# Moving the statistics tile ahead of the activations in SBUF, in a two-block transformer kernel on one core

## What is computed

```python
# first block, once
h = rmsnorm(x, norm_mix_g); u = h @ w_in                 # 1024 x 5376
o_a = rwkv7_time_mix(u[:, :1792], ...)                    # 256 x 512
o_b = diff_attention(u[:, 1792:3328], ...)                # 256 x 512
g_a, g_b = split(sigmoid(u[:, 3328:]))
x = x + (g_a * (o_a @ w_proj_a) + g_b * (o_b @ w_proj_b)) @ w_out
x = x + square(relu(rmsnorm(x) @ w_ff1)) @ w_ff2          # 1024 x 4096 x 1024
x = x + (p @ w_ple) * sigmoid(rmsnorm(x) @ w_ple_gate)
x = rmsnorm(x, final_norm_g)
# second block, two layers
x = x + 0.5 * swiglu(rms_norm(x), gate, up, down)         # 1024 x 2816, twice, x 1024
x = x + mix(rms_norm(x) @ w_in_ab or w_in_cd) @ w_out_2   # attention, 16 heads of 64
x = x + 0.5 * swiglu(rms_norm(x), gate, up, down)
```

## The kernel before

| tile | from byte | modulo 256 |
|---|---|---|
| raw, hi, lo (nine of 8192 bytes) | 0 | 0 |
| X | 73728 | 0 |
| h | 81920 | 0 |
| cols, const | 98304, 98816 | 0, 0 |
| small | 110144 | 64 |
| st (1408 bytes) | 118144 | 128 |
| RB, nt, arena | 119552, 120576, 124672 | 0 |

## Time and profile before

### The profile page before, as it was taken

How to read it: one execution, slowest core, us unless ns; L and a number is a source line. 1 busy time by engine, 2 the same in 40 slices (tenths; PEclk the granted TensorE clock), 3 DMA queues, 4 the chain that set the end, 5 groups by cost and what they waited for, 6 DMA issues and landing times.

```text
span 1466.1 us, 22896 instructions
## 1 busy us (share of the span) xinstructions
PE 1439.1 (98%) x9382; PEld 1233.7 (84%) x9382; DVE 1012.8 (69%) x1339; ACT 767.8 (52%) x1044; POOL 29.6 (2%) x96
## 2 busy tenths in 40 slices
PE   7999999999999999999999999999999999999999
PEld 6999988888887788888878888888888887788887
DVE  5785667787446787647776877468774688687753
ACT  5844365554335565435675555355553456565542
POOL 0000000000001200000000000000000000000000
PEclk9999999999999999999999999999999999999999
DMA  8441124555553465554424555545555454255552
GB/s 312 160 173 60 60 88 169 202 205 196 198 200 145 145 229 175 198 197 156 165 87 145 202 199 176 197 163 211 176 198 195 147 179 146 82 203 199 178 196 86
DMA packets 35815, 249.11 MB, mean 170 GB/s; under 512 B 4096, under 2 KB 4224, under 8 KB 6144
## 3 DMA queue, kind: packets, MB, share of 16 engines
q1 hardware_dynamic: 35712, 247.65, 47.6%
HBM read 246.59 MB, written 1.05 MB: 169 GB/s over the span
## 4 chain that ended last, share of the span: by engine, by line
PE 65%; DVE 1%; ACT 1%; issue 0%; POOL 0%; DVEq 0%; ACTq 0%; POOLq 0%
PE ps L1842 19%; PE ps L1801 10%; PE ps L1841 9%; PE ps L1803 9%; PE ps L1802 9%; PE ps L1838 3%; PE ps L1839 1%; PE ps L2145 1%; PE ps L2125 1%; PE ps L1871 1%; PE ps L2134 0%; PE ps L2074 0%; DVE lo L2494 0%; PE ps L2107 0%; DVE X L2543 0%
## 5 line engine op out<-in xcount | busy, mean ns | idle before, releaser
L2494 DVE TENSOR_TENSOR lo<-raw,hi 128x2048 fp32r<-128x2048 f32 x230 | 526.3, 2290 | 237.0 <-ACT hi L2173 236.7
L2173 ACT CAST hi<-raw 128x2048 fp32r<-128x2048 f32 x230 | 439.1, 1910 | 241.2 <-PE ps L1803 238.1
L1842 PE MATMUL ps<-h,hi 128*128 128x512 f32 x1456 | 519.5, 396 | 0.0
L1841 PE MATMUL ps<-h,lo 128*128 128x256 f32 x1456 | 406.7, 279 | 0.8 <-DVE h L2518 0.8
L1842 PEld LDWEIGHTS ps<-h,hi 128*128 128x128 f32 x1456 | 273.3, 188 | 56.2
L1841 PEld LDWEIGHTS ps<-h,lo 128*128 128x128 f32 x1456 | 274.6, 189 | 10.6 <-DVE h L2518 1.1
L1801 PE MATMUL ps<-hi,a 128*128 128x512 f32 x584 | 230.3, 394 | 0.0
L1803 PE MATMUL ps<-hi,a 128*128 128x512 f32 x584 | 227.6, 390 | 0.0
L1802 PE MATMUL ps<-lo,a 128*128 128x512 f32 x584 | 227.4, 389 | 0.0
L2358 ACT COPY a<-ps 128x256 f32<-128x256 f32 x208 | 76.4, 373 | 204.3 <-PE ps L1842 198.9
L1801 PEld LDWEIGHTS ps<-hi,a 128*128 128x128 f32 x584 | 109.7, 188 | 23.7 <-issue 2.2
(11 more groups left out here) (328 smaller groups left out, 1590.2 us busy)
## 6 DMA issues: line engine op xcount, KB each, us to landing
raw<-ws SPq DMA_DIRECT2D x230, 1024.0 KB, 4.8
X<-xin SPq DMA_DIRECT2D x8, 256.0 KB, 6.3
const<-const SPq DMA_DIRECT2D x1, 1352.0 KB, 11.3
out<-X SPq DMA_DIRECT2D x4, 256.0 KB, 2.1
small<-small SPq DMA_DIRECT2D x1, 992.5 KB, 13.1
a<-row SPq DMA_DIRECT2D x1, 512.0 KB, 5.9
a<-pin SPq DMA_DIRECT2D x1, 256.0 KB, 5.1
const<-const SPq DMA_DIRECT2D x1, 64.0 KB, 2.3
```

What stands on the lines that cost most here:

```text
L1841: e.matmul(b2(sl)[:, 0, :], wl[:, k, a:a + 128], HH[:, k, :], start=False, stop=False)
L1842: t = e.matmul(b2(sl), wh[:, k, a:a + 128], h2[:, k, :, :], start=False, stop=k == 7)
L2173: e.copy(hi[j % NSPL][:, :], raw[j % NRAW][:, :]).then_inc(hi_ready, 1)
L2494: e.tensor_tensor(lo[j % NSPL][:, :], raw[j % NRAW][:, :], hi[j % NSPL][:, :].bitcast(F), ALU.subtract).then_inc(lo_ready, 1)
```

## The change

The line that allocates `st`, the small tile of row statistics and scalars, moves up by five tiles, from behind `small` to ahead of `h`. `h`, `cols`, `const` and `small` each move up by its 1408 bytes, which is 128 modulo 256. `h` begins at 83328 (128 modulo 256), `cols` and `const` too are at 128, `small` at 192, `st` at 0. `raw`, `hi`, `lo`, `X`, `RB`, `nt` and the whole arena stay where they were. No instruction is added, removed or reordered.

```diff
         X = fixed("X", [128, 2, D])
+        st = fixed("st", [128, 352])
         h2 = fixed("h", [128, 8, 2, S], R)
         HH, HL = h2[:, :, 0, :], h2[:, :, 1, :]
         cols = fixed("cols", [128, NCOL])
         const = fixed("const", [128, NK])
         small = fixed("small", [128, NS_])
-        st = fixed("st", [128, 352])
         RB = fixed("RB", [128, S])
```

## The result

Median 1470.61 us (1469.27 to 1471.65, 18 runs) against 1468.13 us before (1466.70 to 1469.25, 18 runs): a ratio of 1.002, 95% interval 1.0014 to 1.0027. The kernel became slower by about 2.5 us. The forecast was 16 us faster.

A forecast was written before the change was run, and what follows sets the result against it. The prediction took TensorE's matmuls to bound the kernel. 16.7 us saved on matmuls reading `h` and weights, less 0.7 us for waits, gave 16.0 us: from 1467.86 to 1451.9 us, by the median 1452 us, range 1429 to 1473 us.

The forecast's parts named there:

- What bounds the kernel: Whole kernel: TensorE, busy 1439.1 of 1466.1 us at full clock, sets the time through the cost of 9382 matmuls.
- The relative address matters, and only to matmuls that read both: `wide`, `cols` and `rows` on `h`: 5056 matmuls reading `h` and weights change pace; products from other tiles keep theirs.
- The rival that nothing would happen: Rival for the whole kernel: the moved address changes no pace, time stays at 1468 us; chance 0.17.
- period 128: Within the no-change rival: addresses may count modulo 128, so the new place of `h` equals the old; 1468 us.
- The price: Matmuls reading `h` and weights: each saves 3.3 ns, `rows` included, 5056 x 3.3 = 16.7 us; chance for 2.2 to 4.4: 0.50.
- The row of `ob`: `cols` on `ob`, 64 bytes off, took 117.8 ns against 120.0 on `oa`: 64 bytes worth 2.2 ns a matmul.
- The streams part wholly: Rival for matmuls on `h`: 6.7 ns saved each, as with 8-column loads, and even passes; 37.5 us, 1430.5 us; chance 0.18.
- Growth with distance: Matmuls on `h`: if savings grow with distance, 128 bytes save twice what 64 do, 4.4 ns each, 22.2 us.
- The worse place: Rival for matmuls on `h`: collision moves somewhere worse; all `wide` passes long, 1471.7 us, or 11.1 us lost, 1479 us; chance 0.15.
- `const`, `small`, `st`: Some 440 matmuls with an operand in `const` or `small`: within 1.3 us either way, taken as 0; `st` operations lie beside matmuls.
- Idle time: TensorE over the whole kernel: its 27 us of idle time may grow but stays below 30 us.
- just-in-time splits: Weight splits just in time, as ahead of L1801 and L1838: waits may grow there, 0.7 us taken off the gain.

The follow-up runs named there:

- e5: Against the kernel before, `st` allocated first of all, so weights and `h` move together by 128 modulo 256 and the arena stays: 1476.94 us, ratio 1.0062.
- e10: Against the kernel before, `h` gets two overlapping places, 192 for the input of `w_in` and 0 for the rest: 1463.39 us, ratio 0.9973.
- e4: Against the kernel before, tiles reordered so that `h` lies at 192 modulo 256 (`small` at 192, `st` at 64): 1466.66 us, ratio 0.9995.
- e1: Against the kernel before, `h` alone moved to 128 modulo 256, every other tile keeping its residue: 1470.56 us, ratio 1.0024.
- e2: Against the kernel before, `h` left in place, `cols`, `const`, `small` and `st` at the residues of the changed kernel: 1467.23 us, ratio 1.0000.
- e3: Against the kernel before, `h` moved to 64 modulo 256, all else keeping its residue: 1468.26 us, ratio 1.0005.
- e9: Model replaced by TensorE alone, one weight pair, `h` moved in 32-byte steps up and down; one trace: at 0, `cols` 120.0 and `rows` 227.1 ns.
- e7: Against the kernel before, `h` and arena tile `s` at 32 modulo 256, arena tile `a` at 96: 1477.83 us, ratio 1.0068.
- e12: TensorE alone, even and odd matmuls alternating operand residues, also shorter loads; one trace: at (0, 0) throughout 227.0 ns for 512 columns, 119.9 for 256.

## Why the prediction was wrong, point by point

- **What bounds the kernel**: right. What the matmuls lose or gain shows up in the time: +2.25 us of paces for +2.5 us, in e5 +9.6 for +9.1 and in e10 -4.7 for -4.0; in e4 -1.7 for -0.7, which the noise covers.
- **The relative address matters, and only to matmuls that read both**: right (e1, e2, e5). The rival that nothing would happen fell, and with it period 128 (e3, e4). The Trainium skill ("SBUF — State Buffer", "Who interferes with whom") says that TensorE never waits on anyone and has two independent read ports, one for the moving operand and one for the load; from this the prediction drew that no address can matter. That conclusion does not hold here: one operand moved by 32 bytes changes the pace of a `rows` matmul from 227.1 to 233.3 ns with no other engine at work (e9). Whether the time goes on a wait between the two reads, so that the page's own sentence fails, is not shown.
- **The price**: this is the step that failed, "I take the middle of the first two, 3.3 ns", and above all "`rows` steps have `h` as the stationary side; I take the same price, for their step over the columns is the same 13.3 ns". The terms were 3328, 1104 and 624 matmuls times -3.3 ns: -11.0, -3.6 and -2.1 us. Measured: +0.55, -0.94 and +2.58 us. The forecast thus had the sign wrong for `rows`, the amount for `cols` (0.9 ns a matmul saved, 3.3 forecast), and for `wide`, two thirds of the matmuls, a gain where there was a small loss. An equal step at distance 0 said nothing on what the step would do elsewhere. For `rows`, 0 is the cheapest distance of the eight tried, for `cols` the dearest (96 beside it, 119.9 ns), for `wide` a middle one (e9).
- **The row of `ob`** was read as a price of 64 bytes. It was one of two rhythms of one distance: `cols` at 64 also ran at 113.3 (e3, e9), and so did `ob` itself with nothing of its own moved (e7). A single stretch, however steady over its 29 triples, can't show that there is a second.
- **The streams part wholly**: not so, and its price had no ground for matmuls of 512 columns. The 6.7 ns came from 256 moving columns; with 512, shorter loads cost more (e12). The reading that the 8-column pace "does not depend on where in 256 bytes these lie" was wrong as well: the earlier trace rows begins behind the first six matmuls of that step, which take 113 to 119 ns.
- **Growth with distance**: no. At 64, 128 and 192 bytes `cols` gains 2.9, 0.9 and 5.6 us, and `rows` loses 3.1, 2.6 and 0.8.
- **The worse place** was the rival on the right side and gave the right test for `rows`; its price, all passes at the longer length, did not occur: they evened out at about 2.80 us. The warning that `wide` might find another rhythm came true. That `cols` falls while `rows` rises was in no case. The measured time lies in the outer range of 1429 to 1473 us by luck: that reached up for no change and for longer passes, and neither is what happened.
- **`const`, `small`, `st`**: the term of 0 was right (e2: 1.0000).
- **Idle time**: right, 28.8 us after 27.0. Of the 1.8 us, 1.3 are the wait for `x` at the start; no other wait grew by more than 0.5. The 0.7 us taken off for just-in-time splits did not show: the waits of L1801 for `lo` sum up to 4.5 us in both profiles.

What stays open is what makes the two operands disturb each other. Shown is that the distance modulo 256 counts, at 32 bytes already, that no other engine is needed for it, and that one distance can have several rhythms. That the load of the next stationary operand collides with the moving stream was the picture behind the forecast; e9 and e12 neither confirm it nor replace it.

## What to carry to other kernels

Measure the distance from start to start of each kind of matmul before putting a price on an address: here one move of `h` by 128 bytes helps `cols`, hurts `rows` and hardly touches `wide`, and a move by 64 gives and takes 3 us, which the time alone doesn't show. Take no price from a single stretch, and none across kinds of different shape or with the operands' roles exchanged. Where tiles serve unlike steps, give each step its own distance rather than looking for one that suits all: the layout with two places gained 0.27% where none of the single places tried in the kernel gained anything that could be measured.

## What was not expected of the hardware

- At the full clock a float32r matmul whose stationary operand is loaded anew costs 6.7 to 13.3 ns beyond 106.7 for 256 columns, and 13.3 to 21 ns beyond 213.3 for 512, by the distance of its operands modulo 256 (e9). In e9, from 18.9 to 21.9 us, matmuls of 512 columns start 427 ns apart, twice 213.3 with nothing over; the record of the granted clock begins only after them.
- With 512 moving columns and operands 0 apart, a load of 64, 32 or 8 stationary columns is dearer than one of 128: 230.0, 231.6 and 231.0 against 227.0 ns (e12).
- One distance can hold two steady paces, 113.3 and 117.8 ns, each kept for a whole stretch (e9, up and down; `ob` in the earlier trace rows and in e7). With 512 columns the pattern (0, 0), (128, 128) ran at 228.2 and at 236.8 ns (e12).
